# Norm roots kept per token and spread by TensorE, and a new order between the first mixer and the first network

## The chip, the cores and the metric

One core of one Trainium2 chip runs the whole computation as one program. The metric is the device time of one execution in microseconds (us), lower is better; the time before is a median of three runs.

## What is computed

Two transformer blocks of depth two each run one after the other on a latent sequence of 256 tokens and, in the first block, a context of 256 tokens; the model is 1024 wide. Every layer is a mixer and then a network, each around a norm:

```python
h = rms_norm(x, g1) * (1 + sc1) + sh1      # sh, sc, gate from silu(c) @ ada_w
x = x + gate1 * y                          # y = mixer(h); first block: gate1 * rms_norm(y)
h = rms_norm(x, g2) * (1 + sc2) + sh2
x = x + gate2 * network(h)
out = rms_norm(x, final_g)                 # after the last layer
# rms_norm(v) = v / sqrt(mean(v * v over the 1024 features) + 1e-6) * g, for each token
```

The first network is a squared-ReLU network over both sequences; the second works on the latent one only; the last two are mixtures of 16 experts.

## The kernel before

Activations lie with the features on the 128 partitions: eight feature tiles (KT = 8) of 256 tokens (SEQ) for each sequence, called CTX (context) and X (own). XT holds x, YT the output y of a mixer or network, HT the scaled x, and RS one row of 256 numbers a sequence, the same on all partitions. PSUM has eight banks of 512 numbers a partition. Weights come in blocks of 128 x 2048 (1 MB) into a ring of four slots, in a fixed order; a block is loaded by SyncE once the block four places ahead of it is used.

Each engine has one queue, written out by hand at the end of the file; semaphore waits name events ("rms", "taken"). A norm goes through these steps. ScalarE squares each tile (`x_squares_scalar`, line 935, or `y_out_scalar`, lines 925 and 927, straight from PSUM). TensorE adds over features with a product against a matrix of ones (`sums_tensor`, line 883), 256 columns of squares moving, so that every partition gets the sum of every token; for some keys GpSimd adds the first six tiles beforehand. The sums of X lie in bank 6, those of CTX in bank 5; where both go together, in one bank. ScalarE takes the root into RS (`root_scalar`, line 907), VectorE inverts all 256 numbers in place (`inverse_root_vector`, line 914), then multiplies. `normed_residual_vector` (lines 1003 and 1008) multiplies y by its inverse root two tiles at a time and adds it into x; `scaled_vector` (line 943) makes HT; `high_scalar` (line 974) rounds it to the fast format and `low_vector` (line 988) makes what the rounding left. Networks multiply in three terms, each over eight tiles (`columns`, line 549): high input with high weights, high input with low weights, low input with high weights.

While a norm is worked out, TensorE issues products that nobody reads (`unread_products`, line 894; five, one, eight or four of them, each 128 x 512 in fp32). `take_bank` makes TensorE wait until the last holder of a bank is marked taken. There are nine seams: before the first network (both sequences, norm of y and norm of x), before the odd recurrence of the first block, before the second network, before the second block's first mixer (each a norm of y and a norm of x), before the two routers, before the odd mixer of the second block, the final norm, and the norms at the very start, which the change leaves alone.

In the first network (`mlp0_tensor`) the first four output tiles are multiplied for X (all three terms), then modulation products (`ahead_mods`, line 614), then for CTX. At the end `final_vector` (line 3810) writes eight tiles and SyncE sends them with one DMA (line 3826).

## Time and profile before

| what | us |
|---|---|
| median of 3 runs | 2351.47 (2351.32 to 2355.02) |
| the profiled execution | 2352.81 |
| its span, first to last instruction | 2350.9 |
| TensorE matmul busy | 2242.8 (95%) |
| VectorE busy | 1427.9 (61%) |
| ScalarE busy | 971.5 (41%) |
| GpSimd busy | 85.4 (4%) |
| mean granted TensorE clock | 0.973 of full |

Times in the rows are us from the span's start. A row of a timeline merges neighbouring instructions of one kind: start, time from the first start to the last end, engine, line, operation, what it writes and reads, its shape, and how many. TensorE's fp32 products show as two records each. Ends of matmuls are modelled and overlap the next start. The granted clock is 1.00 at 2.4 GHz and 0.50 at 1.2 GHz.

### The profile page before, as it was taken

What the parts mean: (1) busy time and instruction counts of PE and PEld (TensorE: products, weight loads), DVE (VectorE), ACT (ScalarE), POOL (GpSimd) and SP (SyncE); (2) the same over time, 40 slices, a digit from 0 to 9 for tenths busy, and PEclk for the clock granted to TensorE, in tenths of its full rate; (3) what the DMA queues carried; (4) which work ended last, traced back from release to release, by engine and by line L of the source; (5) the groups of instructions that cost most, each with busy time, mean ns of one, the idle gap of its engine ahead of it and who ended that gap; (6) DMA issues with size and microseconds to landing.
All of it is one profiled execution on the core that took longest, in us unless ns stands there. A gap on an engine that the chain in (4) does not pass through costs nothing.

```text
span 2350.9 us, 48675 instructions
## 1 busy us (share of the span) xinstructions
PE 2242.8 (95%) x21596; PEld 1852.2 (79%) x21596; DVE 1427.9 (61%) x2467; ACT 971.5 (41%) x1716; POOL 85.4 (4%) x83
## 2 busy tenths in 40 slices
PE   8999999999999999999999999998999999899997
PEld 5864478888867789999998899895677879677786
DVE  3273536867657366887763653465475876656576
ACT  2244333332313223433322563344355655545565
POOL 1000000000010000000000001020000002000000
PEclk9999999999999989999999999998999999999999
DMA  8335237656522100000003446444355853204484
GB/s 355 108 111 213 89 128 302 252 214 233 215 99 104 40 1 4 4 4 4 13 4 129 142 176 239 197 180 179 126 219 210 337 218 126 72 1 179 177 339 181
DMA packets 47314, 348.13 MB, mean 148 GB/s; under 512 B 5264, under 2 KB 5280, under 8 KB 5760
## 3 DMA queue, kind: packets, MB, share of 16 engines
q1 hardware_dynamic: 45936, 334.52, 37.8%
q0 software_dynamic: 1168, 10.50, 1.1%
q8 instruction: 170, 2.79, 0.5%
q14 instruction: 40, 0.33, 0.0%
HBM read 343.95 MB, written 1.05 MB: 147 GB/s over the span
## 4 chain that ended last, share of the span: by engine, by line
PE 52%; DVE 8%; ACT 3%; issue 1%; DVEq 0%; ACTq 0%
PE banks L549 10%; PE banks L2245 6%; PE banks L2257 5%; PE banks L1037 4%; PE banks L3179 3%; PE banks L3180 3%; PE banks L3181 3%; PE banks L3210 2%; PE banks L3212 2%; PE banks L3211 2%; PE banks L2097 1%; PE banks L2304 1%; PE banks L561 1%; PE banks L2279 1%; PE banks L3228 1%
## 5 line engine op out<-in xcount | busy, mean ns | idle before, releaser
L527 DVE TENSOR_TENSOR mlp_w_low<-weight_slots,mlp_w_high 128x2048 fp32r<-128x2048 f32 x64 | 146.5, 2289 | 186.8 <-ACT mlp_w_high L518 186.8
L527 DVE TENSOR_TENSOR moe_w_low<-weight_slots,moe_w_high 128x2048 fp32r<-128x2048 f32 x96 | 217.9, 2289 | 61.6 <-ACT moe_w_high L518 60.8
L518 ACT ACTIVATE mlp_w_high<-weight_slots 128x2048 fp32r<-128x2048 f32 x64 | 122.4, 1912 | 177.8 <-PE banks L549 122.6
L518 ACT ACTIVATE moe_w_high<-weight_slots 128x2048 fp32r<-128x2048 f32 x96 | 181.7, 1914 | 23.6 <-PE banks L3212 19.8
L1037 PE MATMUL banks<-arena,weight_slots 128*128 128x256 f32 (+1 forms) x512 | 140.7, 436 | 3.0 <-DVE arena L2846 1.5
L3179 PE MATMUL banks<-moe_w_high,slots_x 128*128 128x512 f32 x320 | 130.6, 408 | 2.8 <-DVE moe_w_low L527 2.8
L1037 PEld LDWEIGHTS banks<-arena,weight_slots 128*128 128x128 f32 x512 | 97.8, 192 | 43.7 <-issue 33.6
L3180 PE MATMUL banks<-moe_w_low,slots_x 128*128 128x512 f32 x320 | 127.6, 399 | 0.0
L3181 PE MATMUL banks<-moe_w_high,slots_x 128*128 128x512 f32 x320 | 127.5, 398 | 0.0
L686 DVE SCALAR_TENSOR_TENSOR arena<-weight_slots,silu_c,arena 128x256 f32<-128x256 f32 x240 | 99.4, 483 | 0.0
L2245 PE MATMUL banks<-arena 64*64 64x64 f32 (+1 forms) x1600 | 81.9, 234 | 0.0
L2245 PEld LDWEIGHTS banks<-arena 64*64 64x64 f32 x1600 | 78.3, 139 | 0.5 <-issue 0.3
L1281 ACT ACTIVATE arena<-arena 128x256 f32<-128x256 f32 (+2 forms) x128 | 62.3, 489 | 38.8 <-DVE arena L1225 38.7
L864 POOL TENSOR_TENSOR arena<-arena 128x256 f32<-128x256 f32 (+1 forms) x30 | 36.5, 1216 | 1031.9 <-ACT arena L1683 407.8
L3179 PEld LDWEIGHTS banks<-moe_w_high,slots_x 128*128 128x128 f32 x320 | 60.7, 190 | 15.8 <-DVE moe_w_low L527 3.2
L3181 PEld LDWEIGHTS banks<-moe_w_high,slots_x 128*128 128x128 f32 x320 | 60.7, 190 | 14.7
L549 PE MATMUL banks<-quarter_high,mlp_w_high 128*128 128x512 f32 x256 | 67.4, 400 | 3.5 <-ACT quarter_high L1674 3.4
L3180 PEld LDWEIGHTS banks<-moe_w_low,slots_x 128*128 128x128 f32 x320 | 60.9, 190 | 12.4
L614 PE MATMUL banks<-weight_slots,arena 128*32 128x256 f32 x896 | 65.1, 414 | 4.5 <-DMA weight_slots<-weights 4.5
L549 PE MATMUL banks<-both_high,mlp_w_high 128*128 128x512 f32 (+1 forms) x288 | 68.3, 375 | 0.9 <-ACT both_high L974 0.8
L2257 PE MATMUL banks<-weight_slots 64*64 64x32 f32 x2048 | 66.6, 221 | 1.2 <-DVE weight_slots L2719 1.2
L2504 ACT ACTIVATE weight_slots<-banks 128x256 f32<-128x256 f32 x64 | 23.0, 382 | 107.7 <-DVE weight_slots L2709 107.2
(454 smaller groups left out, 5211.1 us busy)
## 6 DMA issues: line engine op xcount, KB each, us to landing
weight_slots<-weights SPq DMA_DIRECT2D x318, 1024.0 KB, 4.9
arena<-small POOLq DMA_DIRECT2D x1, 2560.0 KB, 9.0
arena<-x_t POOLq DMA_DIRECT2D x1, 2048.0 KB, 12.8
arena<-bias POOLq DMA_DIRECT2D x1, 2048.0 KB, 11.4
constants<-consts POOLq DMA_DIRECT2D x1, 1395.0 KB, 17.9
out_t<-arena SPq DMA_DIRECT2D x1, 1024.0 KB, 3.9
parameters<-params POOLq DMA_DIRECT2D x1, 763.0 KB, 21.8
arena<-pool_inv POOLq DMA_DIRECT2D x1, 512.0 KB, 14.6
```

The costliest lines, as they stand in the source:

```text
L518: nc.scalar.activation(self.pair(j)[0], slot(j, 0, SLOT), ACT.Copy).then_inc(*act.step("high", j))
L527: nc.vector.tensor_tensor(self.pair(j)[1], slot(j, 0, SLOT), self.pair(j)[0], ALU.subtract).then_inc(*v.step("used", j))
L549: ins = nc.tensor.matmul(out, self.pair(j)[part][:, at:at + P], x(k), start=start and n == 0 and k == 0, stop=stop and n == 2 and k == til ...
L614: ins = nc.tensor.matmul(psum(7, n % 2 * 256, 256, slice(32 * g, 32 * g + 32)), Z[:, 22 + 32 * k - n // 2 * 2:][:, 0:32], slot(j, k, 256), ...
L686: nc.vector.scalar_tensor_tensor(a_, w, c, a_, ALU.mult, ALU.add).then_inc(*v.step())
L1037: ins = nc.tensor.matmul(psum(b, 0, w), slot(j, k, 256, i * P, P), moving(k), start=(k == 0), stop=(k == KT - 1))
L1281: nc.scalar.activation(S[:, u % N, c:c + w], S[:, u % N, c:c + w], ACT.Exp, bias=M[:, u % N, 3 + j:4 + j], accum_out=M[:, u % N, 6 + j:7 + ...
L2245: ins = nc.tensor.matmul(psum(b, n * width, width, r), lhs, rhs, start=(i == 0), stop=(i == len(ts) - 1))
L2257: ins = nc.tensor.matmul(psum(b, p * 32, 32, half(h)), lhs(p, half(h)), rhs(p, half(h)), start=opens, stop=True, skip_group_check=True)
L3179: nc.tensor.matmul(psum(b), x_hi, wh, start=(k == 0), stop=False)
L3180: nc.tensor.matmul(psum(b), x_hi, wl, start=False, stop=False)
L3181: ins = nc.tensor.matmul(psum(b), x_lo, wh, start=False, stop=(k == KT - 1))
```

## The change

For X everywhere, and for CTX in the norms before the first network, sum and root are kept per token, with the tokens on the partitions. The sums come from products whose stationary operand is the squares (128 tokens at a time) and whose moving operand is one column of ones, so they are two columns. Root and reciprocal work on 128 x 2 numbers. Then TensorE spreads them over the partitions (`spread_root_tensor`): the column, repeated, is the stationary operand, the identity moves, twice 128 columns, into the upper half of the bank that held the sums. VectorE reads the inverse roots from PSUM there and marks that bank taken when it has read them for the last time. The unread products are divided over the new places.

Before the first network, VectorE now does: both inverse roots, the own residual, two tiles of the context's residual, the own scaling, the other six tiles, the own low parts, and then the context's scaling and low parts. ScalarE rounds the own part before it squares the context. TensorE multiplies the own part's two high terms for four output tiles, then the low terms, then modulations, then the context's sums and spread, then the context's part. The result leaves in four DMAs of two tiles.

```diff
@@ -536,10 +536,11 @@
                 return j
 
             def columns(self, pe, j, width, a, out, tiles, high, low, start=True, stop=True, check=False, norm=None, seg=None,
-                        parts=None):
+                        parts=None, only=(0, 1, 2)):
 
                 terms = [(0, high, "h_high"), (1, high, None), (0, low, "h_low")]
-                for n, (part, x, ready) in enumerate(terms):
+                for n in only:
+                    part, x, ready = terms[n]
                     for k in range(tiles):
...
@@ -864,6 +865,27 @@
                 nc.gpsimd.tensor_tensor(total, total, squares_of(key, segs, k), ALU.add).then_inc(*g_.step())
             g_.mark("squares_added", key)
 
+        def by_token(key, seg):
+
+            return seg == X or key in ("y_x01", "n2_0")
+
+        def root_at(key, seg):
+            return {("y_x01", X): 2, ("y_x02", X): SEQ}.get((key, seg), 0)
+
+        def spread_root_tensor(pe, key, seg):
+
+
+            b = take_bank(pe, ("spread", key, seg), [SUMS_BANK[seg]])
+            pe.wait_ge(*after("inverse_root", key, seg))
+            for t in range(2):
+                ins = nc.tensor.matmul(psum(b, SEQ + t * P, P), RS[:, seg, t:t + 1].to_broadcast([P, P]), cn("ident"),
+                                       start=True, stop=True)
+            ins.then_inc(*pe.step("rms", key, seg))
+
+        def inverse_roots(key, seg):
+
+            return psum(bank_of(("spread", key, seg)), SEQ, SEQ) if by_token(key, seg) else RS[:, seg, :]
+
         def sums_tensor(pe, key, segs, k):
...
@@ -880,8 +902,17 @@
             else:
                 pe.wait_ge(*after("square", key, segs[0], k))
                 k_at = k
-            ins = nc.tensor.matmul(psum(SUMS_BANK[segs[-1]], 0, len(segs) * SEQ), cn("ones"), squares_of(key, segs, k_at),
-                                   start=opens, stop=(k == KT - 1))
+            squares = squares_of(key, segs, k_at)
+            for i, seg in enumerate(segs):
+                x = squares[:, i, :] if len(segs) == 2 else squares
+                at, b = root_at(key, seg), SUMS_BANK[segs[-1]]
+                if by_token(key, seg):
+                    for t in range(2):
+                        ins = nc.tensor.matmul(psum(b, at + t, 1), x[:, t * P:(t + 1) * P], cn("ones", 0, 1),
+                                               start=opens and i == 0 and t == 0, stop=(k == KT - 1), skip_group_check=True)
+                else:
+                    ins = nc.tensor.matmul(psum(b, at, SEQ), cn("ones"), x, start=opens and i == 0, stop=(k == KT - 1),
+                                           skip_group_check=True)
             if k == KT - 1:
                 ins.then_inc(*pe.step("sums", key, segs[-1]))
                 if len(segs) == 2:
...
-            nc.scalar.activation(RS[:, seg, :], psum(bank_of(("sums", key, seg)), at, SEQ), ACT.Sqrt,
+            w = 2 if by_token(key, seg) else SEQ
+            nc.scalar.activation(RS[:, seg, 0:w], psum(bank_of(("sums", key, seg)), root_at(key, seg), w), ACT.Sqrt,
                                  bias=cn("eps", 0, 1), scale=1.0 / D).then_inc(*act.step("root", key, seg))
             act.mark("taken", "sums", key, seg)
 
         def inverse_root_vector(v, key, seg):
 
             v.wait_ge(*after("root", key, seg))
-            nc.vector.reciprocal(RS[:, seg, :], RS[:, seg, :]).then_inc(*v.step("rms", key, seg))
+            if by_token(key, seg):
+                part = RS[:, seg, 0:2]
+                nc.vector.reciprocal(part, part).then_inc(*v.step("inverse_root", key, seg))
+            else:
+                nc.vector.reciprocal(RS[:, seg, :], RS[:, seg, :]).then_inc(*v.step("rms", key, seg))
 
         def y_out_scalar(act, key, segs, then=None):
...
+                                               mod_col(m, 3 * half + 1, k, seg), inverse_roots(key, seg),
                                                ALU.mult, ALU.mult).then_inc(*v.step("scaled", key, k, seg))
+            if by_token(key, seg):
+                v.mark("taken", "spread", key, seg)
 
...
+        def normed_residual_vector(v, key, m, half, seg, x=XT, tiles=(0, KT)):
 
             v.stage("residual")
             v.wait_ge(*after("mod_ready", m, mod_part(m, 1)))
             v.wait_ge(*after("rms", "y_" + key, seg))
-            r = RS[:, seg, :].unsqueeze(1).to_broadcast([P, 2, SEQ])
+            r = inverse_roots("y_" + key, seg).unsqueeze(1).to_broadcast([P, 2, SEQ])
             made = {}
-            for k in range(0, KT + 2, 2):
-                if k < KT:
+            for k in range(tiles[0], tiles[1] + 2, 2):
+                if k < tiles[1]:
                     y = YT[:, seg, k:k + 2, :]
                     nc.vector.tensor_tensor(y, y, r, ALU.mult).then_inc(*v.step())
                     made[k] = v.own
-                if k >= 2:
+                    if k == KT - 2 and by_token("y_" + key, seg):
+                        v.mark("taken", "spread", "y_" + key, seg)
+                if k > tiles[0]:
                     v.wait_ge(*made[k - 2])
...
                     for f in range(4):
-                        take_bank(pe, ("x02_up", f))
-                    for seg in (X, CTX):
+                        take_bank(pe, ("x02_up", f), range(4))
+
+                    def part(seg, f, only):
+                        return MLP0.columns(pe, first[f // 2], 256, f % 2 * P, psum(bank_of(("x02_up", f)), seg * SEQ, SEQ), KT,
+                                            lambda k: XHI2[:, seg, k, :], lambda k: XLO2[:, seg, k, :], norm="n2_0",
+                                            seg=seg, only=only)
+                    for only in ((0, 1), (2,)):
                         for f in range(4):
-                            j = first[f // 2]
-                            ins = MLP0.columns(pe, j, 256, f % 2 * P, psum(bank_of(("x02_up", f)), seg * SEQ, SEQ), KT,
-                                               lambda k: XHI2[:, seg, k, :], lambda k: XLO2[:, seg, k, :], norm="n2_0",
-                                               seg=seg)
-                            if seg == CTX:
-                                ins.then_inc(*pe.step("x02_up", f))
-                                if f % 2:
-                                    pe.mark("multiplied", j)
-                        if seg == X:
-                            ahead_mods(pe)
+                            part(X, f, only)
+                    ahead_mods(pe)
+                    x_sums_tensor(pe, "n2_0", [CTX])
+                    spread_root_tensor(pe, "n2_0", CTX)
+                    pe.stage("mlp_up0")
+                    for f in range(4):
+                        part(CTX, f, (0, 1, 2)).then_inc(*pe.step("x02_up", f))
+                        if f % 2:
+                            pe.mark("multiplied", first[f // 2])
                 for c in range(2 if q == 0 else 0, 4):
...
             start = block_of[f"moe{l}"][0]
-            unread_products(pe, 4, 0)
+            unread_products(pe, 2, 0)
+            spread_root_tensor(pe, f"n2_{l + 2}", X)
+            unread_products(pe, 1, 0)
...
-                nc.vector.scalar_tensor_tensor(HT[:, X, k, :], XT[:, X, k, :], pr("final_g2", k, 1), RS[:, X, :],
+                nc.vector.scalar_tensor_tensor(HT[:, X, k, :], XT[:, X, k, :], pr("final_g2", k, 1), inverse_roots("final", X),
                                                ALU.mult, ALU.mult).then_inc(*v.step("final", k))
...
             load_blocks(sp)
-            for k in range(KT):
+            for k in (1, 3, 5, 7):
                 sp.wait_ge(*after("final", k))
-            eng.dma_start(out_t, HT[:, X].rearrange("p a b -> p (a b)")).then_inc(*sp.step(by=16, sem="out_written"))
+                eng.dma_start(out_t[:, (k - 1) * SEQ:(k + 1) * SEQ], HT[:, X, k - 1:k + 1].rearrange("p a b -> p (a b)")).then_inc(
+                    *sp.step(by=16, sem="out_written"))
             sp.wait_ge(*sp.own)
 
...
-            x_sums_tensor(pe, "n2_0", [X, CTX], 5)
-            unread_products(pe, 1, 0)
+            unread_products(pe, 2, 0)
+            for seg in (X, CTX):
+                spread_root_tensor(pe, "y_x01", seg)
+            unread_products(pe, 3, 0)
+            x_sums_tensor(pe, "n2_0", [X])
+            unread_products(pe, 2, 0)
+            spread_root_tensor(pe, "n2_0", X)
             mlp0_tensor(pe)
-            x_sums_tensor(pe, "n1_1", ONE, 5)
-            unread_products(pe, 8, 0)
+            unread_products(pe, 2, 0)
+            spread_root_tensor(pe, "y_x02", X)
+            unread_products(pe, 3, 0)
...
                        lambda: compressed_turned(pe))
@@ -3911,6 +3978,7 @@
                            banks=range(6), then=x_sums(pe, "n2_3"))
             moe_tensor(pe, 1)
             x_sums_tensor(pe, "final", ONE)
+            spread_root_tensor(pe, "final", X)
 
         @block.scalar
...
+            root_scalar(act, "y_x01", X)
             root_scalar(act, "y_x01", CTX)
-            x_squares_scalar(act, "n2_0", "x01", X)
-            root_scalar(act, "n2_0", X)
-            x_squares_scalar(act, "n2_0", "x01", CTX)
-            root_scalar(act, "n2_0", CTX)
             for seg in (X, CTX):
+                x_squares_scalar(act, "n2_0", "x01", seg)
+                root_scalar(act, "n2_0", seg)
                 high_scalar(act, "n2_0", 0, 1, [seg], BOTH)
             mlp0_scalar(act)
-            root_scalar(act, "y_x02", X, SEQ)
...
                 inverse_root_vector(v, "y_x01", seg)
-                normed_residual_vector(v, "x01", 0, 0, seg)
-            for seg in (X, CTX):
-                inverse_root_vector(v, "n2_0", seg)
-                scaled_vector(v, "n2_0", 0, 1, seg)
-                low_vector(v, "n2_0", 0, 1, [seg], BOTH)
+            normed_residual_vector(v, "x01", 0, 0, X)
+            normed_residual_vector(v, "x01", 0, 0, CTX, tiles=(0, 2))
+            v.stage("norm")
+            inverse_root_vector(v, "n2_0", X)
+            scaled_vector(v, "n2_0", 0, 1, X)
+            normed_residual_vector(v, "x01", 0, 0, CTX, tiles=(2, KT))
+            v.stage("norm")
+            low_vector(v, "n2_0", 0, 1, [X], BOTH)
+            inverse_root_vector(v, "n2_0", CTX)
+            scaled_vector(v, "n2_0", 0, 1, CTX)
+            low_vector(v, "n2_0", 0, 1, [CTX], BOTH)
```

The other two-root seams are changed as the one of "y_x01" and "n2_0" is: two unread products, spread, three unread, x sums, two unread, spread, then one (before the odd recurrence four). The seam before the odd mixer has two unread, spread, one. `scaled_vector` and `final_vector` take the inverse roots from `inverse_roots`.

## Rows read from the trace of the kernel before

**Rows 1.** Page, busy us (share of the span) and instructions
```profile
PE 2242.8 (95%) x21596; PEld 1852.2 (79%) x21596; DVE 1427.9 (61%) x2467; ACT 971.5 (41%) x1716; POOL 85.4 (4%) x83
```
**Rows 2.** Line 914: count, ns min/median/max, first and last start
```profile
L914 DVE RECIPROCAL arena<-arena x16: 1743/1753/1754, 269.2 to 2341.5; 128x256 f32<-128x256 f32 x16
```
**Rows 3.** Timeline, TensorE, seam before the second network: start us, us, what
```profile
1296.98 4.45 PE L894 MATMUL banks<-constants 128*128 128x512 f32 x10
...
1306.29 3.60 PE L894 MATMUL banks<-constants 128*128 128x512 f32 x8
...
1309.96 3.09 PE L549 MATMUL banks<-h_high,mlp_w_high 128*128 128x256 f32 x8
```
**Rows 4.** Timeline, VectorE, the same seam
```profile
1299.48 1.29 DVE L1003 TENSOR_TENSOR arena<-arena 128x512 f32<-128x512 f32 x2
...
1302.88 0.68 DVE L1003 TENSOR_TENSOR arena<-arena 128x512 f32<-128x512 f32 x1
...
1308.79 3.26 DVE L943 SCALAR_TENSOR_TENSOR arena<-arena,modulations 128x256 f32<-128x256 f32 x8
```
**Rows 5.** Timeline, ScalarE, the same seam
```profile
1303.99 1.61 ACT L935 ACTIVATE arena<-arena 128x256 f32<-128x256 f32 x4 [0.58 <-DVE arena L1008]
```
**Rows 6.** Timeline, TensorE, products with one moving column
```profile
381.88 1.03 PE L704 MATMUL banks<-constants,arena 128*128 128x1 f32 x8
382.77 2.11 PE L549 MATMUL banks<-quarter_high,mlp_w_high 128*128 128x512 f32 x8
```
**Rows 7.** End of the kernel: timelines of four engines, windows
```profile
2336.12 3.23 DVE L3421 SCALAR_TENSOR_TENSOR arena<-banks,modulations,arena 128x256 f32<-128x256 f32 x8 [0.84 <-PE banks L3228]
...
2343.30 3.26 DVE L3810 SCALAR_TENSOR_TENSOR arena<-arena,parameters 128x256 f32<-128x256 f32 x8
...
2341.00 0.47 ACT L907 ACTIVATE arena<-banks,constants 128x256 f32<-128x256 f32 x1 [1.21 <-PE banks L883]
...
2337.35 3.61 PE L883 MATMUL banks<-arena,constants 128*128 128x256 f32 x16
...
2346.65 0.35 SPq L3826 DMA_DIRECT2D out_t<-arena  x1
...
2347.40:2350.10 2.70, 0.00 (x0) 0.00 (x0) 0.00 (x0) 0.00 (x0) 0.00 (x0) 0.50 0.94 388
```
**Rows 8.** Timelines at the first router: short instructions of three engines
```profile
1706.92 0.20 ACT L779 ACTIVATE table_touch<-constants 128x1 f32<-128x1 f32 x1
...
1705.16 0.16 DVE L3294 TENSOR_REDUCE arena<-arena 128x2 f32<-128x8 f32 x1
...
1700.17 0.30 PE L3114 MATMUL banks<-constants,arena 128*128 128x128 f32 x1
```
**Rows 9.** Timeline, TensorE, seam before the first network
```profile
268.50 4.45 PE L894 MATMUL banks<-constants 128*128 128x512 f32 x10
...
287.02 3.25 PE L549 MATMUL banks<-both_high,mlp_w_high 128*128 128x256 f32 x8 [0.76 <-ACT both_high L974]
...
290.07 1.91 PE L549 MATMUL banks<-both_high,mlp_w_low 128*128 128x256 f32 x8
...
293.37 1.12 PE L549 MATMUL banks<-both_high,mlp_w_high 128*128 128x256 f32 x8
...
302.10 1.07 PE L614 MATMUL banks<-weight_slots,arena 128*32 128x256 f32 x16
...
314.71 2.00 PE L549 MATMUL banks<-both_high,mlp_w_high 128*128 128x512 f32 x8
```
**Rows 10.** Timeline of TensorE and windows, compressed keys of the sparse attention
```profile
2015.16 3.75 PE L3683 MATMUL banks<-arena 64*128 64x15 f32 x64
...
2028.06 2.07 PE L1102 MATMUL banks<-constants 128*128 128x512 f32 x2
...
2016.00:2020.00 4.00, 3.45 (x61) 3.25 (x60) 1.01 (x3) 0.71 (x4) 0.00 (x0) 1.00 0.49 203
...
2020.00:2024.00 4.00, 0.69 (x2) 0.29 (x2) 3.76 (x13) 2.91 (x11) 0.00 (x0) 0.55 0.00 0
```

More of the change, by code:

```diff
@@ L894, in unread_products, with x_sums_tensor @@
                 nc.tensor.matmul(psum(bank), cn("ones"), CN[:, 0:512], start=True, stop=True)
-        def x_sums_tensor(pe, key, segs, unread=0):
+        def x_sums_tensor(pe, key, segs):
             pe.stage("norm")
-            if unread:
-                unread_products(pe, unread, 0)
             for seg in segs:
@@ L991, in low_vector @@
                     v.mark("h_low", key, k)
-        def normed_residual_vector(v, key, m, half, seg, x=XT):
+        def normed_residual_vector(v, key, m, half, seg, x=XT, tiles=(0, KT)):
             v.stage("residual")
@@ L3883, in _ @@
                            banks=range(6), then=y_sums(pe, "x11", ONE))
-            x_sums_tensor(pe, "n2_1", ONE, 5)
-            unread_products(pe, 4, 0)
-            mlp_split_tensor(pe)
-            x_sums_tensor(pe, "n1_2", ONE, 5)
-            unread_products(pe, 4, 0)
+            unread_products(pe, 2, 0)
+            spread_root_tensor(pe, "y_x11", X)
+            unread_products(pe, 3, 0)
+            x_sums_tensor(pe, "n2_1", ONE)
+            unread_products(pe, 2, 0)
+            spread_root_tensor(pe, "n2_1", X)
+            unread_products(pe, 1, 0)
+            mlp_split_tensor(pe)
+            unread_products(pe, 2, 0)
+            spread_root_tensor(pe, "y_x12", X)
+            unread_products(pe, 3, 0)
+            x_sums_tensor(pe, "n1_2", ONE)
+            unread_products(pe, 2, 0)
+            spread_root_tensor(pe, "n1_2", X)
+            unread_products(pe, 1, 0)
             ev2_tensor(pe)
@@ L3905, in _ @@
             x_sums_tensor(pe, "n1_3", ONE)
-            unread_products(pe, 4, 0)
+            unread_products(pe, 2, 0)
+            spread_root_tensor(pe, "n1_3", X)
+            unread_products(pe, 1, 0)
             od_tensor(pe)
```

9 lines of the change are left out of this document (6 added, 3 removed).

## The prediction

> **What bounds the kernel now.** I read the page first, then the timeline of each engine around every norm, since the change touches nothing else. TensorE is busy for 95% of the span [rows 1], so the network and projection stages run at its pace. A norm is a seam in that work: squares on ScalarE, sums over the features on TensorE, root on ScalarE, reciprocal and scaling on VectorE, rounding on ScalarE, and only then the next products. All 16 full-width reciprocals take about 1.75 us [rows 2]. What the reader must see next is that TensorE isn't idle in a seam: it issues products whose result nobody reads (line 894). The clean example is the seam before the second network [rows 3, 4, 5]. Call T the moment the y sums leave TensorE's queue, 1296.98. Five unread products take 4.45 us, 0.89 each. VectorE's first multiply comes at T+2.50. Its fourth ends at 1302.88 + 0.68, T+6.6. ScalarE's last squares end at 1303.99 + 1.61, and the x sums are out 0.7 behind them at 1306.29, T+9.3; scaling starts at T+11.8 (2.50 behind the sums again); the first rounded product comes at T+13.0.
>
> **Part 1, roots per token.** A sum becomes two products with one moving column for each feature tile, in place of one with 256. Eight records of the nearest kind (four such products) took 1.03 us including the drain of the last [rows 6]; the next line started 0.89 us after them, so I take 0.22 us a product. Eight feature tiles cost 16 x 0.22 = 3.5 us, against 3.6 for 16 records before [rows 7]. A gain of nothing, but no loss either.
>
> Root and reciprocal of two columns: the nearest ScalarE instruction takes 0.20 us and the nearest VectorE one 0.16 [rows 8]; with 0.05 for each handover the pair takes 0.5 us in place of 2.3. That is 1.8 us a norm on paper. It is not to be had, because in TensorE's queue two unread products, 2 x 0.89 = 1.78 us, now stand ahead of the products that spread the root. Those are two fp32 products of 128 columns, a quarter of 0.89 each, 0.43 together, and the last record ends 0.30 after its start [rows 8], about 0.2 behind the queue. So 1.78 + 0.43 + 0.2 + 0.1 handover = 2.5 us from the end of the sums to VectorE, against 2.50 before. Bounds: 0.75 (nothing ahead, as at the very end of the kernel) and 2.5. I take 2.5 wherever two unread products stand there. The scaling reads the root from PSUM instead of SBUF: eight such instructions take 3.23 us with a PSUM operand (line 3421) and 3.26 without (line 3810) [rows 7], so zero.
>
> **A wait that the change adds.** The spread root lies in the same PSUM bank as the sums. The x sums must now wait until VectorE has read the y root for the fourth multiply, T+6.6; before, they followed the squares one by one. What is queued behind them on TensorE is the whole seam. They start at T+6.8 and take 3.5, so they end at T+10.3, not T+9.3. This costs 1.0 us in each of the three seams with two roots (before the odd recurrence of the first block, the second network, the second block's first mixer): **+3.0**. Between zero (squares were the limit) and 1.3 each.
>
> **Part 2, single seams.** At the two routers the order is unread 2, spread, unread 1: 3.1 us where four unread took 3.6, and scaling is no earlier. Router products start 0.15 us earlier each: **-0.3**. The seam before the odd mixer: **0**.
>
> **Part 3, the first network.** This seam stands in [rows 9]. Before, VectorE did all of both residuals, then both scalings, and the own part began on TensorE at 287.02. With T = 268.5 and the steps above, the own sums end at 278.8 (T+10.3), scaling starts at 281.3, and products 1.2 behind it as in [rows 3, 4], at 282.5: 4.5 us earlier. The own part is then a group of eight held to the rounding's pace (3.25 us), seven more and four low groups at 0.96 each (nine groups stand between 293.37 and 302.10), 13.8 us, covering the context residual and the low parts; it ends at 296.3. The next weights' modulation products (1.07) end at 297.4. Only now come the context's sums, 3.5 us on TensorE's own time, where before they were in the shadow. Then root, reciprocal and spread with nothing to overlap, 0.2 + 0.2 + 0.75 + handovers, a scaling and a rounding: first context product at 303.5. Before it was 303.1 and everything it needed was there. Now the first group is again held for 3.25 instead of 0.96 us, and the low part of the context, made on VectorE after its scaling (two passes of 3.26), holds the third group until 309.1. Three more trios of 2.88 end at 317.7; before, the context part ended at 314.7. **+3.0**. If the low part did not hold it: +1.6; if sums wait on more: +4. Nothing later absorbs it: the next weight transfers are released by TensorE's own use of the slots.
>
> **Part 4, the end.** No unread product stands there. The root starts at 2341.00; 0.2 + 0.16 + 0.75 for load and spread + handovers give scaling at 2342.5, not 2343.30: -0.8. The output's packets filled the stretch from 2347.4 to 2350.1, its issue stands at 2346.65 [rows 7]: 0.85 us behind the issue, 2.5 us of data. The last quarter has a quarter of the data, the other three move while VectorE makes the next pair (0.79 us), and one issue costs SyncE 0.35: -1.8, between -1.9 and 0 (if small packets cost as much as large). Together **-2.6**. The Trainium skill, "DMA: Bandwidth & Descriptors", Rules for kernel authors, speaks against this edit: many small transfers should be coalesced into one. By its fixed cost of about 2.0 us for a transfer the last quarter would land some 2.6 us after its issue, an estimate, and the edit would save about 1.3; the sum goes by the rows above.
>
> Sum so far: 3.0 + 3.0 - 0.3 - 2.6 = **+3.1 us**, with TensorE at full clock.
>
> **The clock.** In the timeline of 2012 to 2032, 64 loads with products of 15 columns and a gap are followed by a granted clock of 0.55, though loads filled 3.25 of 4 us; an unread product there takes twice the 0.89-1.1 us of the others (2.07) [rows 10]. In the first network's seam eight products spread over 3.25 us are followed by slow ones, 1.91 in place of 1.12 [rows 9]. So narrow products and gaps, the loads notwithstanding, preceded 1.2 GHz. The x sums were until now 3.4 us of 256-column products; they become 3.5 us of one-column products behind a wait of up to 1.9. If these don't hold the clock, the unread and spread products after them (2.2 us at 2.4 GHz, 4.4 at 1.2) stand on the path. A slow stretch covering about half of them costs 1.1 us: three seams 3.3, odd mixer 0.7, and in the first network three places (before the own part, its first groups, the context's first groups) 2.5. **+6.5**, bounds 0 and 12. The Trainium skill, "TensorE: Matmul & The Clock Gate", The HAM clock gate, says that activity releases the throttle and idleness sets it; it doesn't say whether loads with one moving column are activity. If they are, the sum is +3.1, if not, +9.6.
>
> The profiled execution took 2352.81 us, its span 2350.9 and 1.9 around it; it is 1.3 above the median of 2351.47. The terms are differences, so I add them to the median: 2351.5 + 9.6 = **2361.1**.
>
> **Rivals.**
> (a) Clock holds: +3.1, 2354.6. For it: loads keep the array's input busy; in the second network's seam the unread products behind the x sums keep 0.90 us each [rows 3]. Against: the fall at 2020, which came behind loads too.
> (b) Faster: the loads for one-column products go at the pace of the 64 in [rows 10], 3.75/64 = 0.058 us each, since nothing moves behind them. The sums then take 1.9 us and are held by squares: each double seam 1.3 less, the first network 2.9 less, odd mixer and end 0.7 each less: 3.1 - 3.9 - 2.9 - 1.4 = -5.1, 2346.4, slightly over 0.2%. It decides when a load costs under 0.08. Against: those loads have 64 rows, and [rows 6] has 0.11 for full ones.
> (c) The fillers leave the path: if they ran beside the roots, the 1.8 us a norm would be real, about -10. Against: one queue, in order. I give it next to nothing.
> (d) The narrow sums cool the clock for longer than half a filler: +12 instead of +6.5, 2366.6.
>
> **Chances.** Forecast 0.50, (a) 0.27, (b) and (c) 0.14, (d) 0.09. 0.2% is 4.7 us, about what a measurement of this kernel can tell from no change. (a) is within it, with some of the forecast's low side (0.02) and of (b); faster 0.12, same 0.30, slower 0.58. Range: 2350.0 to 2365.5 holds (a) and the forecast with its bounds; the forecast's own is 2356 to 2365.5.
>
> **What would show it.** Reciprocals of two columns near 0.16 us; L883's group at 0.44 us a tile, its first one directly behind the fourth multiply; VectorE's first multiply still 2.5 us behind the y sums; own products of the first network 4 us earlier, context products ending 3 us later; granted clock below 1 around each line-894 group that follows x sums; scaling at the end 0.8 us and the output 1.8 us shorter. I am wrong if those groups stay at 0.89 us a product, or if the sums take under 3 us.

## The result and the profile after

The changed kernel takes 2369.4 us (median of five runs, 2367.4 to 2378.1); the kernel before took 2353.0 beside it (2351.3 to 2355.0). The ratio is 1.0075, 95% interval 1.0062 to 1.0089: 16 us slower. The forecast was 2361.1, with a range up to 2365.5: the sign was right, the size was not.

The page after has two lines to lay beside [rows 1] (in the second, each digit is TensorE's granted clock in one of 40 equal slices of the span, in tenths). VectorE gave back 23 us of busy time, and TensorE, the bound, took 16 us more. Its mean granted clock fell from 0.973 to 0.963. At two levels, 1.00 and 0.50, a mean of 0.973 is 2 x 0.027 x 2351 = 127 us at 1.2 GHz, one of 0.963 is 175 us.

```profile
PE 2259.2 (95%) x21806; PEld 1878.9 (79%) x21806; DVE 1405.1 (59%) x2467; ACT 968.2 (41%) x1716; POOL 84.3 (4%) x83
...
PEclk8999999999999989999999999999999999999999
```

The reciprocals of two columns (count, ns min/median/max) take a tenth of those in [rows 2], as forecast. Two full ones remain, those of the context in the seam before the odd recurrence, where the change keeps sum and root of the context as they were.

```profile
L946 DVE RECIPROCAL arena<-arena x14: 165/166/166, 270.1 to 2360.1; 128x2 f32<-128x2 f32 x14
```
```profile
L948 DVE RECIPROCAL arena<-arena x2: 1743/1744/1746, 718.4 to 733.3; 128x256 f32<-128x256 f32 x2
```

TensorE's timeline in the seam before the second network, the one in [rows 3] (L911 sums, L925 unread products, L881 spread):

```profile
1310.57 1.96 PE L925 MATMUL banks<-constants 128*128 128x512 f32 x4
1312.37 0.61 PE L881 MATMUL banks<-constants,arena 128*128 128x128 f32 x4
1312.82 2.74 PE L925 MATMUL banks<-constants 128*128 128x512 f32 x6
1317.13 5.69 PE L911 MATMUL banks<-constants,arena 128*128 128x1 f32 x32 [1.58 <-DVE arena L1039]
1322.68 3.76 PE L925 MATMUL banks<-constants 128*128 128x512 f32 x4
1326.24 1.06 PE L881 MATMUL banks<-constants,arena 128*128 128x128 f32 x4
```

VectorE there, and windows over the seam (us; busy time and count of PE, PEld, DVE, ACT, POOL; granted clock; DMA share; GB/s):

```profile
1313.02 1.29 DVE L1039 TENSOR_TENSOR arena<-arena,banks 128x512 f32<-128x512 f32 x2 [1.81 <-PE banks L881]
...
1327.34 3.22 DVE L977 SCALAR_TENSOR_TENSOR arena<-arena,modulations,banks 128x256 f32<-128x256 f32 x8 [4.02 <-PE banks L881]
```
```profile
1308.00:1316.00 8.00, 7.56 (x33) 4.64 (x31) 3.25 (x9) 1.73 (x5) 0.00 (x0) 1.00 0.69 261
1316.00:1324.00 8.00, 6.87 (x34) 6.35 (x35) 2.83 (x8) 2.68 (x7) 0.00 (x0) 0.66 0.00 1
1324.00:1330.00 6.00, 4.98 (x9) 1.88 (x8) 2.66 (x7) 2.15 (x6) 0.00 (x0) 0.60 0.01 3
```

T is 1310.57. The first multiply is at T+2.45 (2.50 before). The x sums start at T+6.56, held by line 1039, the fourth multiply: the added wait on the bank of the spread root, as forecast. Then the clock falls, and what the forecast had at full rate takes longer: the sums 5.7 us (3.5 forecast), two unread products 3.76 (1.88 in e3, the experiment below that keeps the clock at 1.00 here), the spread 1.06 (0.61). Scaling starts at T+16.8, not T+12.8.

The first network, TensorE, beside [rows 9]:

```profile
281.30 3.47 PE L925 MATMUL banks<-constants 128*128 128x512 f32 x4
...
286.39 3.38 PE L550 MATMUL banks<-both_high,mlp_w_high 128*128 128x256 f32 x8 [1.18 <-ACT both_high L1010]
...
301.92 4.36 PE L911 MATMUL banks<-constants,arena 128*128 128x1 f32 x32
306.92 1.19 PE L881 MATMUL banks<-constants,arena 128*128 128x128 f32 x4 [0.65 <-DVE arena L946]
309.23 3.37 PE L550 MATMUL banks<-both_high,mlp_w_high 128*128 128x256 f32 x8 [1.11 <-ACT both_high L1010]
```

The own part begins 0.6 us earlier than before, the context part 6 later. The end of the kernel, beside [rows 7]:

```profile
2360.12 0.17 DVE L946 RECIPROCAL arena<-arena 128x2 f32<-128x2 f32 x1 [1.98 <-ACT arena L937]
...
2361.67 3.22 DVE L3854 SCALAR_TENSOR_TENSOR arena<-arena,parameters,banks 128x256 f32<-128x256 f32 x8 [1.38 <-PE banks L881]
2362.57 2.68 SPq L3870 DMA_DIRECT2D out_t<-arena  x4
```

**Where the time went.** Lag is how much later TensorE's same product starts in one profile than in that of before. Stretches are given in us of before; the columns are what each adds to the lag.

| stretch | forecast, without and with clock | after | e3, sums with 128 columns |
|---|---|---|---|
| start to 260 | 0 | +1.2 | -0.1 |
| first network, 260 to 360 | +3.0, +5.5 | +9.5 | +3.5 |
| before the odd recurrence, to 711 | +1.0, +2.1 | +3.3 | +2.5 |
| key products, 722 to 745 | 0 | -6.6 | -6.7 |
| recurrence, 745 to 1290 | 0 | +6.3 | +6.2 |
| before the second network, to 1330 | +1.0, +2.1 | +4.9 | +0.7 |
| before the second block's mixer, 1507 to 1529 | +1.0, +2.1 | +4.1 | +1.4 |
| routers and experts, 1529 to 1740 | -0.3 | -4.1 | -4.0 |
| odd mixer, 1912 to 1924 | 0, +0.7 | +2.7 | +0.2 |
| the rest to 2337 | 0 | -2.3 | +0.3 |
| end | -2.6 | -2.1 | -2.5 |

(The forecast shared the clock's 3.3 us over three seams alike.)

The two large rows in which the change does nothing, the recurrence and the routers, go with the clock. From 745 to 1290 us the mean granted clock is 0.95 before, 0.94 after and in e3, 0.96 in e1 (-0.6 us) and 0.97 in e7 (-4.7 us); from 1529 to 1740 us it is 0.94 before and in e1 (-0.2), 0.96 after and 0.97 in e3. One hundredth less over 545 us is 11 us more at 1.2 GHz, about 5.5 us lost.

### The profile page after: what moved, and what is told of

The parts are those of the page before. It is cut to its first block, busy times and chain, and to the rows that moved or that the text cites. A ratio compares the mean times of both kernels' runs of the same rounds, so it can differ in the third digit from the quotient of the medians.

```text
span 2367.6 us, 49102 instructions
## 1 busy us (share of the span) xinstructions
PE 2259.2 (95%) x21806; PEld 1878.9 (79%) x21806; DVE 1405.1 (59%) x2467; ACT 968.2 (41%) x1716; POOL 84.3 (4%) x83
## 4 chain that ended last, share of the span: by engine, by line
PE 85%; DVE 9%; ACT 4%; issue 1%; DMA 1%; DVEq 0%; ACTq 0%
PE banks L550 27%; PE banks L1075 6%; PE banks L2287 6%; PE banks L2299 5%; PE banks L3223 3%; PE banks L3225 3%; PE banks L3224 3%; PE banks L2139 3%; PE banks L1897 2%; PE banks L615 2%; PE banks L3254 2%; PE banks L911 2%; PE banks L3256 2%; PE banks L3255 2%; PE banks L925 1%; PE banks L2346 1%
## 5 line engine op out<-in xcount | busy, mean ns | idle before, releaser
L2287 PE MATMUL banks<-weight_slots,arena 64*64 64x64 f32 (+1 forms) x1088 | 67.2, 250 | 0.0
L2287 PE MATMUL banks<-arena,weight_slots 64*64 64x64 f32 x960 | 67.0, 222 | 0.0
```

The costliest lines, as they stand in the source:

```text
L2287: ins = nc.tensor.matmul(psum(b, n * width, width, r), lhs, rhs, start=(i == 0), stop=(i == len(ts) - 1))
```

## The experiments

Each is compared with runs of the kernel before that were taken beside it (medians 2351.9, 2352.6 and 2353.0 us for the three groups e1 to e4, e5 to e8, e9 to e12).

**e1_rot_after and e2_rot_before: the order in which banks are taken.** The table has -6.6 us in products that the change does not touch. `spread_root_tensor` calls `take_bank`, which moves on one counter for all pools, so every later product lands in other banks. e1 gives the kernel before only that, e2 takes only that back from the changed one.

```diff
 # e1, at each place where the change has spreads (4, 2, 2, 2, 1, and 1 in each router)
             unread_products(pe, 1, 0)
+            bank_state["next"] += 4
             mlp0_tensor(pe)
 # e2, in spread_root_tensor
             b = take_bank(pe, ("spread", key, seg), [SUMS_BANK[seg]])
+            bank_state["next"] -= 1
```

> The kernel before, with nothing changed but the count by which TensorE picks the next PSUM bank: it is moved on by the number of spreads that the change adds (4, 2, 2, 2, 1, 1 and 1 at the seams), so that every later product takes the bank it takes in the changed kernel. The changed kernel gains 6.6 us between 722 and 760 us and loses some 6 us in the recurrence (760 to 1290). Theory R, the bank rotation did both: this kernel shows the same two steps, so about 0 in sum. Theory C, the clock and chance did them: this kernel is at the time of before within 1 us everywhere.

> The changed kernel with the bank count set back by one after each spread, so that every product outside the seams takes the bank of the kernel before. Theory R: the 6.6 us gained after 722 us are lost again and those of the recurrence come back, the seams stay as they are; 2369 +- 2. Theory C: same as the changed kernel everywhere.

e1: 2345.6 us (10 runs), ratio 0.9971, interval 0.9961 to 0.9981. e2: 2376.4 (4 runs), ratio 1.0103, 1.008 to 1.0125. The place, TensorE, in the kernel before, in e2, in the changed kernel, and in e1 (no wait behind the unread products in the last two):

```profile
728.98 2.74 PE L894 MATMUL banks<-constants 128*128 128x512 f32 x6
736.55 7.32 PE L1855 MATMUL banks<-mix_k_high,wk_w_high 128*128 128x512 f32 x24 [4.83 <-ACT arena L1496]
```
```profile
743.99 2.74 PE L926 MATMUL banks<-constants 128*128 128x512 f32 x6
751.57 7.64 PE L1898 MATMUL banks<-mix_k_high,wk_w_high 128*128 128x512 f32 x24 [4.85 <-ACT arena L1535]
```
```profile
742.98 2.74 PE L925 MATMUL banks<-constants 128*128 128x512 f32 x6
745.15 6.09 PE L1897 MATMUL banks<-mix_k_high,wk_w_high 128*128 128x512 f32 x24
```
```profile
727.50 2.74 PE L894 MATMUL banks<-constants 128*128 128x512 f32 x6
729.68 6.06 PE L1855 MATMUL banks<-mix_k_high,wk_w_high 128*128 128x512 f32 x24
```

With the old count the key products' first bank is one that ScalarE reads late, and TensorE stands 4.85 us. This part of the change is a gain of 6 to 7 us that has nothing to do with norms. Without it the change costs 1.0%. Only this half of theory R holds. In e1 the recurrence takes as long as before (-0.6), so the bank order alone does not cause the changed kernel's 6.3 there. e2 has +1.8 in it and ended 7 us above its forecast of 2369.

**e3_wide_sums: the clock.** The sums keep their form, but move all 128 columns of ones, not one; the root reads one column of the result. All else is the changed kernel.

```diff
-matmul(psum(b, at + t, 1), x[:, t * P:(t + 1) * P], cn("ones", 0, 1), ...)
+matmul(psum(b, at + t * P, P), x[:, t * P:(t + 1) * P], cn("ones"), ...)
```

> The changed kernel with 128 columns of ones moving in the sums instead of one; the sums are the same numbers, 128 times over, and the root reads one column of each 128. A product of 128 columns in fp32 streams for about 0.22 us, what its weight load takes anyway. Theory K (the narrow sums cool the clock, and the price is the slow sums, unread products and spreads): granted clock 1.00 behind the x sums, sums of eight tiles in 3.5 us instead of 3.9 to 5.6, two unread products in 1.8 instead of 3.4 to 3.6; the seams cost 1.0 each (first network about 3.5), the time falls by 12 to 18 us to 2352 to 2357. Theory W (waits and order alone cost the time): within 2 us of the changed kernel.

2354.4 us (2347.0 to 2359.2, 10 runs), ratio 1.0007, 0.9995 to 1.0018: 15 us under the changed kernel and within the forecast, by giving TensorE 128 times the columns in these products. The seam before the second network, timeline and window:

```profile
1308.97 3.84 PE L911 MATMUL banks<-constants,arena 128*128 128x128 f32 x32 [1.58 <-DVE arena L1042]
1312.65 1.88 PE L925 MATMUL banks<-constants 128*128 128x512 f32 x4
1314.37 0.61 PE L881 MATMUL banks<-constants,arena 128*128 128x128 f32 x4
```
```profile
1310.00:1316.00 6.00, 5.83 (x36) 4.05 (x34) 1.66 (x6) 1.69 (x6) 0.00 (x0) 1.00 0.00 0
```

The same order, the same wait (1.58 us), and a clock of 1.00 where the changed kernel had 0.66 and 0.60. The seams' losses fall to between +0.2 and +3.5 (last column of the table). The loads alone were no less busy in the changed kernel: 6.35 of 8 us in its window at 0.66. So loads for one moving column do not hold the clock here. The Trainium skill, "TensorE: Matmul & The Clock Gate", The HAM clock gate, says that the clock is set by how busy the array has been lately. It does not say how loads with one moving column count; in these rows the clock fell behind them.

**e4_split_out: the output in four transfers**, alone in the kernel before.

```diff
-            for k in range(KT):
+            for k in (1, 3, 5, 7):
                 sp.wait_ge(*after("final", k))
-            eng.dma_start(out_t, HT[:, X]...)
+                eng.dma_start(out_t[:, (k - 1) * SEQ:(k + 1) * SEQ], HT[:, X, k - 1:k + 1]...)
```

> The kernel before with its output sent in four DMAs of two tiles instead of one. By the packets of the profile it should be 1.8 us faster at the end (the last DMA's packets fill 0.7 us instead of 2.5); if each transfer had its own fixed cost one behind the other, 0 to 1 us slower.

2352.0 us (10 runs), ratio 1.0002, 0.9992 to 1.0011: the timing can't tell 1.8 us from nothing. In the profile, the stretch from TensorE's last product ahead of the final sums (2337.2 in the kernel before) to the end takes 12.0 us, against 13.7 in each of the three profiles with one transfer (before, e1, e11): 1.7 us shorter. That is about what the forecast gave the split (1.8) and somewhat over its estimate of 1.3 from the fixed cost in the Trainium skill, "DMA: Bandwidth & Descriptors", Anatomy of one DMA. One of the four transfers takes 2.3 us from issue to landing, by the profile.

**e5_wide_old_order: the order of the first network.** e3 with the order of before: both sums, both spreads, both scalings, then the own and the context part.

```diff
-            x_sums_tensor(pe, "n2_0", [X])
-            unread_products(pe, 2, 0)
-            spread_root_tensor(pe, "n2_0", X)
+            x_sums_tensor(pe, "n2_0", [X, CTX])
+            for seg in (X, CTX):
+                spread_root_tensor(pe, "n2_0", seg)
             mlp0_tensor(pe)
```

> The wide-sums kernel with the first network's order of before: both residuals, both short reciprocals, then both scalings; sums of both sequences and both spreads on TensorE ahead of the own part; all three terms of the own part, modulations, context part. Theory O (the context's sums and chain on TensorE's own time cost the first network its 3.5 us): the lag at 360 us goes from +3.5 to -1 us against the kernel before, and the time is 4 to 5 us under the wide-sums kernel. If the order does not matter: within 1.5 us.

e5 also takes the network's first output banks from the whole pool again, where the changed kernel takes them from 0 to 3.

2356.5 us, ratio 1.0015, 1.0005 to 1.0024, and +6.6 us between 260 and 360. It does not answer the question, since it brought a wait of its own:

```profile
284.94 0.68 PE L881 MATMUL banks<-constants,arena 128*128 128x128 f32 x4 [0.20 <-DVE arena L949]
294.36 2.07 PE L550 MATMUL banks<-both_high,mlp_w_high 128*128 128x256 f32 x8 [8.73 <-DVE arena L980]
```

The first output bank was the one with the context's spread root, which VectorE reads until its last scaling (line 980). TensorE stood 8.7 us. e9 mends this.

**e6_wide_other_bank: the wait on the spread's bank.** e3, with the y roots of the three two-root seams spread into bank 5, so that the x sums in bank 6 need not wait for the fourth multiply.

```diff
-            b = take_bank(pe, ("spread", key, seg), [SUMS_BANK[seg]])
+            b = take_bank(pe, ("spread", key, seg), [SUMS_BANK[CTX] if key in ("y_x02", "y_x11", "y_x12") else SUMS_BANK[seg]])
```

> The wide-sums kernel with the spread roots of y in bank 5 instead of the sums' bank 6 in the three seams with one sequence and two roots, so that the x sums no longer wait until VectorE has read them. Theory B (the wait costs 1.0 us a seam): x sums start with the first squares and end 0.7 us behind the last, scaling 1.0 us earlier in each of the three seams, 3 us in all. Otherwise nothing.

2347.7 us (2339.5 to 2352.6), ratio 0.9976, 0.9962 to 0.9989. TensorE:

```profile
1306.59 2.35 PE L911 MATMUL banks<-constants,arena 128*128 128x128 f32 x16
1309.17 2.05 PE L911 MATMUL banks<-constants,arena 128*128 128x128 f32 x16 [0.23 <-ACT arena L972]
```

The 1.58 us of idle time is gone, the sums start early and wait on squares for 0.23. The three seams cost -0.2, -0.2 and +0.7 where e3 had +0.8, +0.7 and +1.4: 0.7 to 1.0 each, against 1.0 forecast. (The first is taken at the first product behind the seam. The rest of the table's +2.5, 1.7 us in e3 and as much in e6, comes behind it: the recurrence's first 64 records take 15.74 us in both, 14.05 before.) The median fell by more than these 3 us; e3's and e6's runs spread over 12 and 13 us, so only the seams' rows are read for size.

**e7_wide_no_filler: are the unread products ahead of a spread on the path?** e3 without the two unread products at ten of the eleven places where they stand ahead of a spread (they stay ahead of the own spread before the first network); those of the y roots stand behind the spread instead.

```diff
-            unread_products(pe, 2, 0)
             spread_root_tensor(pe, "y_x11", X)
-            unread_products(pe, 3, 0)
+            unread_products(pe, 5, 0)
```

> The wide-sums kernel without the two unread products ahead of the spreads (those of y stand behind the spread instead), at ten of the twelve places. Theory F (the fillers stand on the path and eat what the short roots gain): VectorE starts 1.3 to 1.4 us behind the sums instead of 2.5, about 1.1 us a place, 8 to 11 us in all, to about 2344, as long as the clock holds. If the root chain is as long as the fillers: no change. If the fillers hold the clock: slow stretches in the seams eat it.

2344.4 us (9 runs), ratio 0.9963, 0.9952 to 0.9973. TensorE before the second network:

```profile
1297.43 3.84 PE L911 MATMUL banks<-constants,arena 128*128 128x128 f32 x32
1301.91 0.68 PE L881 MATMUL banks<-constants,arena 128*128 128x128 f32 x4 [0.64 <-DVE arena L949]
```

Root and reciprocal are an idle gap of 0.64 us; the two unread products took 1.8 in that place. By VectorE's timeline its first scaling there starts at 1302.64, 1.5 us behind the sums; in e3 it is 2.4. So the fillers are on the path, as the forecast had it, but are worth 0.8 us a place and not their own 1.8, since root and reciprocal ran beside them.

The median is that of the forecast, and in part by luck. The seam before the second block's mixer went from +1.4 to -0.9, the odd mixer's from +0.2 to -0.7, but the one before the second network only from +0.7 to +0.1: the products behind it now run at a granted clock of 0.72 (1306 to 1312 us), where those behind the same seam in e3 have 1.00. Of the 14.2 us between the two profiles at 2337, 10.9 are the recurrence, where e7 ran at 0.97 and e3 at 0.94 and the edit does nothing.

**e8_all: e5, e6 and e7 together.**

> All three edits together on the wide-sums kernel: order of before in the first network, y spreads in the other bank, no unread product ahead of ten spreads. If they add: 4.5 + 3 + 10 under the wide-sums kernel, about 2337.

2343.6 us (5 runs), ratio 0.9960, 0.9946 to 0.9974, with the same 8.7 us of waiting as e5 and 6 to 7 us over the forecast.

**e9 to e12: the order again, with output banks 0 to 3.** e9 is e5 with `take_bank(pe, ("x02_up", f), range(4))`. e10 is e8 with it. e11 is e1 with only the changed kernel's first network, full-width sums and roots kept. e12 is e9 with one-column sums. (e11 also takes its output banks from 0 to 3, where e1 has the whole pool; neither waits for a bank there.)

> The changed kernel with 128 moving columns in the sums (as e3), and the first network in the order of before: both residuals, both own and context sums, both scalings, then the own part and the context part; its four output banks are taken from banks 0 to 3, so that none is the bank of a spread root (in e5 that bank cost 8.7 us of waiting). Theory O (the new order costs what the prediction's part 3 says, some 3 to 4 us, because the context's sums, roots and rounding now stand uncovered between the two parts): the lag behind the kernel before is between -1.5 and +0.5 us at 360 us, where e3 had +3.5, and the whole is 3 to 5 us under e3. Rival P (the order is free, what e3 lost there comes from the wait of the context's sums for the spread's bank): the lag at 360 stays at +3 or more.

> e9, and the roots of the three two-root seams spread into the other bank (as e6), and no unread products ahead of a spread (as e7). If the three savings add up (about 1 us a seam for the bank, 1 us a seam for the unread products, 4 us for the order), the lag at 2337 us is under that of e8 by the 8.7 us of bank wait less what the order saved there, and the median is 2335 to 2341 us, under both kernels by more than 0.4%. Rival: the places that are left without unread products turn cold, or the seams are then held by VectorE and ScalarE; then it stays at 2343 or above.

> The kernel before with full-width sums and roots, the bank count of after (as e1), and only the new order of the first network: own scaling before the rest of the context's residual, own products first in their two high terms, context sums in TensorE's queue behind the own part. Theory O: the lag at 360 us is +3.5 to +5 (the 3.0 of part 3, and about 1.1 more, since root and reciprocal of 256 numbers take 2.3 us there and nothing covers them), the rest follows e1; about 2349 to 2351 us. Rival P (the order is worth nothing or gains, since the own products start 4 us earlier): the lag at 360 is under +1 and the time is e1's, 2346.

> The changed kernel with its one-column sums, but the order of before in the first network, output banks 0 to 3. It splits the 9.5 us that the changed kernel loses between 260 and 360 us. If order and cold clock add (order 3.5 as e3 showed, clock 6), the loss there is 5 to 7 us, and the whole is 3 to 5 us under the changed kernel, 2364 to 2366 us. If the new order multiplies the clock's cost (three places where it turns cold in place of one, the context's sums and spread uncovered), the loss is only 2 to 4 us and the whole 2360 to 2363 us.

Medians: e9 2346.8 us (10 runs), ratio 0.9977, 0.9964 to 0.9990; e10 2336.7 (4 runs), 0.9932, 0.9911 to 0.9952; e11 2353.2 (10 runs), 1.0002, 0.9993 to 1.0012; e12 2367.6 (4 runs), 1.0068, 1.0043 to 1.0094. With e1 and e3 they fill a square. Lag added between 260 and 360 us, with the mean granted clock of that stretch (0.97 before):

| sums and roots | order of before | new order | the order costs |
|---|---|---|---|
| full width | -0.6 at 0.97 (e1) | +6.7 at 0.91 (e11) | 7.3 |
| per token, 128 columns move | -3.2 at 1.00 (e9) | +3.5 at 0.97 (e3) | 6.7 |
| per token, one column moves | +4.1 at 0.88 (e12) | +9.5 at 0.88 (changed kernel) | 5.4 |

Each cell is one profile, and the spread between profiles is not small: e6 has e3's instructions in this stretch and adds +6.6 at a clock of 0.93, e7 +6.2 at 0.93. A hundredth of clock over 100 us is about 1 us. So of the order's cost, up to 6 of the 7.3 us and 3 of the 6.7 are clock, and so is the whole difference between e1 and e9 in the old order. The medians of whole kernels agree that the order costs: 7.6 us from e1 to e11, and 7 us by the ratios of e9 and e3. From e12 to the changed kernel it is only 1.8, with intervals that overlap.

e11's rows, TensorE (its y sums leave the queue at 267.91):

```profile
282.37 3.28 PE L550 MATMUL banks<-both_high,mlp_w_high 128*128 128x256 f32 x8 [2.71 <-ACT both_high L975]
...
298.49 3.72 PE L884 MATMUL banks<-arena,constants 128*128 128x256 f32 x16
305.62 3.38 PE L550 MATMUL banks<-both_high,mlp_w_high 128*128 128x256 f32 x8 [3.41 <-ACT both_high L975]
308.80 1.91 PE L550 MATMUL banks<-both_high,mlp_w_low 128*128 128x256 f32 x8
310.50 1.91 PE L550 MATMUL banks<-both_low,mlp_w_high 128*128 128x256 f32 x8
```

and e9's (268.55):

```profile
286.12 3.19 PE L550 MATMUL banks<-both_high,mlp_w_high 128*128 128x256 f32 x8 [0.29 <-ACT both_high L1013]
...
300.36 1.07 PE L615 MATMUL banks<-weight_slots,arena 128*32 128x256 f32 x16
301.36 1.21 PE L550 MATMUL banks<-both_high,mlp_w_high 128*128 128x256 f32 x8
```

In the old order the context's scaling and rounding lie behind the own products, and the context part follows with no gap. In the new one its sums (3.7), an idle gap (3.4), a first group at the pace of rounding (3.38 us, 1.21 in e9), and two more at a lower clock (1.91 each for 1.12) stand on the path. And e12's two sets of sums, the first at a granted clock of 1.00 (277.7 to 281.4 us), the second at 0.50 (283.3 to 290.2 us):

```profile
277.76 3.73 PE L911 MATMUL banks<-constants,arena 128*128 128x1 f32 x32 [0.59 <-DVE arena L1039]
283.32 6.99 PE L911 MATMUL banks<-constants,arena 128*128 128x1 f32 x32 [1.83 <-DVE arena L1039]
```

Of the four forecasts, e10's held. e9 lost less in the first network than forecast (-3.2, between -1.5 and +0.5 forecast) and is 7 us under e3, not 3 to 5. e11 lost more (+6.7, at most +5 forecast) and ended at 2353.2, not 2349 to 2351. e12 met neither of its two: its +4.1 lies between "order and clock add" (5 to 7) and "they multiply" (2 to 4), and its 2367.6 above both.

e10, 128 columns in the sums, the old order, the other bank and no filler ahead of ten spreads, is 0.7% faster than the kernel before and 33 us faster than the changed one. Its parts are known from e1 and e9: the bank count alone gives 0.9971, and e9, which adds per-token roots and the split output to it in the old order, gives no more (0.9977). What brings e10 to 0.9932 is the other bank and the missing fillers, about 10 us. What the missing fillers would give with full-width roots was not tried.

## Why the prediction was off, step by step

- **Price of the sums (3.5 us): right at 2.4 GHz only.** With one moving column they took 3.6 to 3.7 at a granted clock of 1.00, and up to 7.0 below it. e3 has 3.84 with 128 columns.
- **Root and reciprocal hidden behind two unread products, 2.5 us: right** (T+2.45). Its lower bound, 0.75 us with nothing ahead, was not: e7 measured 1.5.
- **The added wait, 1.0 in each of three seams: right** in place and nearly in size (0.7 to 1.0, e6).
- **The first network, +3.0: near as a total (+3.5 in e3), and in part by luck.** e6, with the same instructions, has +6.6. In e3 the own products start at 282.25 (282.5 forecast) and the context's at 303.2 (303.5 forecast). But the context's first three groups then take 3.38, 1.91 and 1.91 us, the last two at a granted clock of 0.50 (304 to 310 us) that part 3 did not have. By 330 us e3 has lost 5.1 us, and it gets 1.6 back around 345, where the trace of before has a slow stretch and e3 none. The forecast also compared the new order only with the kernel before, never with the old order under the new roots. There (e9) TensorE starts the own part at 286.1 and goes on to the context part without a gap.
- **The clock, +6.5: the step that failed.** Its mechanism was right, and e3 shows it. Its size was not: "a slow stretch covering about half of" the unread and spread products. In the seam before the second network the sums themselves turn slow (5.7 for 3.5), and the unread and spread products behind them in full, 2.3 us more and not 1.1. The changed kernel less e3 is 6.0 in the first network, 0.8, 4.2, 2.7 and 2.5 in the others, 16.2 together, and 15.0 between the medians. (Less e6, the first network's part is 2.9 and not 6.0, so the seams' sum is good to about 3 us.) The bound of 12 was too low for the same reason, and the range's upper end, 2365.5, left out even what that bound gives, 2366.6.
- **The key products, -6.6: not foreseen.** The rotation of banks through `take_bank` is in the diff and in no term of the sum. The wait of 4.8 us that it removed lay in the trace of before, in a stretch where the prediction did not look. It hid part of the clock's cost.
- **The recurrence, +6.3: not foreseen; the clock is its size, its cause stays open.** The change does nothing there. Kernels with the same instructions in it gained or lost between -4.7 (e7) and +6.3 us in their profiles, roughly in step with the clock granted there (0.97 to 0.94). e3 has nearly the same +6.2 as the changed kernel, so it is not the narrow sums, and e1 has -0.6, so it is not the bank order alone. All profiles with full-width roots stay within 1 us, those with per-token roots lie on both sides; what decides where the slow stretches fall was not isolated. The routers' -4.1 (-4.0 in e3) is of the same sort.
- **The end, -2.6: right** (-2.1, and -2.5 in e3; of it -1.7 for the split, by e4).

Rival (a), the clock holds in the seams, is what e3 measures when it is made true: +2.6 us against 3.1 forecast. The match is partly luck, since e3's sum holds -6.7 and -4.0 and +6.2 that no term had. Rival (b), faster loads, is out: 32 records in 3.6 to 3.7 us at full clock are 0.11 each. Rival (c) is out by e7, where taking the fillers from the queue brought VectorE's start forward. Rival (d), more cooling than half a filler, was the real one, and its 2366.6 still fell short.

## What to carry over

Here, replacing wide products by narrow ones saved TensorE nothing, since each needed its own full load, and it took the clock from what stood behind it: price the following instructions at 1.2 GHz too, the narrow ones included. A change of order is to be compared with the old order under all other edits, for two edits in one seam can hide each other's sign. And any edit that takes a bank, a slot or a counter from a shared rotation moves waits far from where it stands; the waits of the whole trace are to be read for holders that will change. And a difference of a few us in one stretch of one profile is to be laid beside the granted clock of that stretch before it is put down to an edit.

## What was not expected of the hardware

- A one-column fp32 product with a 128 x 128 load costs about the same as one with 128 columns at 2.4 GHz: 32 records in 3.63 (changed kernel) and 3.73 us (e12) against 3.84 (e3). At 1.2 GHz the former rise to 6.99 for 32 (e12).
- In the seam before the second network, loads with one column moving behind each fell into a granted clock of 0.66 and were followed by 0.60, though loads were busy for 6.35 of 8 us; the same loads with 128 columns (e3) kept 1.00.
- Four output transfers of 256 KB issued 0.8 us apart ended the kernel 1.7 us sooner than one of 1 MB issued last (12.0 us behind the last common product in e4, 13.7 in three profiles with one transfer).
- The same instructions differ between profiles by as much as the effects studied here: -4.7 to +6.3 us in a recurrence of 545 us, at mean granted clocks of 0.97 to 0.94.
